# Interleaving the first convolution products with the input transposes, moving the token weights' low halves to VectorE, and splitting extra expert tiles two ahead

## The chip, the cores and the metric

The kernel runs on one core of one Trainium2 chip. A core has TensorE (PE: matmuls, and PEld: its weight loads), VectorE (DVE), ScalarE (ACT), GpSimd (POOL) and SyncE (SP, which here only issues DMAs). Each engine works through its own list of instructions in order; semaphores make one wait for another. The metric is the device time of one execution in microseconds (us); of several runs the median counts.

## What is computed

One step of a one-layer decoder over 1024 prompt tokens and 64 sample tokens, with 1024 channels. Cut to what the change touches:

```python
xn = rmsnorm(h, g_mix)
z = xn @ w_in                                  # columns: q, k, v, og, lr (tokens) and cv (convolution)
q, k, v, og, lr, cv = jnp.split(z, SPLITS, axis=-1)
...                                            # gated linear attention (GLA) from q, k, v, og, lr
a, gate = jnp.split(cv, 2, axis=-1)
u = a * jax.nn.sigmoid(gate)
c, buf_new = causal_depthwise_conv(u, buf0, w_conv, b_conv)     # 31 taps for each of 512 channels
c = jax.nn.silu(layernorm(c, g_conv_ln, b_conv_ln))
h = h + jnp.concatenate([o, c], axis=-1) @ w_out
xn = rmsnorm(h, g_ffn)
h = h + hier_moe(xn, ...)                      # 32 experts, two for each token
h = h + sigmoid(rmsnorm(h, g_ple) @ w_ple_gate) * (p_l @ w_ple_proj)
```

## The kernel before

The tokens are padded to 1152 and worked on in 9 tiles of 128. Products that need more accuracy than one 16-bit product are made of three: each operand is split into a high half (its value in 16 bits) and a low half (the rest), and the passes (high, high), (high, low), (low, high) are added up in PSUM. A split is thus two instructions: a copy (ACT) and a subtraction (DVE or POOL).

**Input stage.** For each tile SP loads 128 rows of x (`load_x`, two in flight), ACT squares and sums them, DVE normalises them (`norm_x`, L1244), PE turns them in eight transposes (`transpose_x`, L1718), ACT copies the high half out of PSUM (`evac_xT`, L892) and DVE subtracts for the low half (L1250). All of PE and DVE first wait for `g1_in`, which counts the load of the gains and of the whole table of constants (704.5 KB).

**Convolution products.** When all nine tiles are turned, PE multiplies four groups c of 128 channels (L1733): for each c two parts (gate and value), three blocks of 384 tokens, eight chunks of channels and three passes, 144 matmuls in all. The weights of a group (`w_cv`, 1 MB) come by DMA into one buffer; ACT makes the high half (L901) and POOL the low half (L713). ACT empties the six blocks of PSUM (L937: sigmoid of the gate, copy of the value) and POOL multiplies the two into `u` (L728, L729).

**Token weights.** The weights of q, k, v, og and lr come in eight chunks k of two halves (776 columns each) through two small buffers, `side`. For each half SP loads (L532), ACT makes the high part (L924), POOL the low part (L718), and only then may SP load the next chunk into that buffer (semaphore `wt_lo`). `w_pieces` puts chunks 0 to 2 into the list of group c=0, 3 to 5 into c=1, 6 and 7 into c=2, on SP, ACT and POOL alike; on ACT they stand ahead of the emptying of that group's PSUM.

**Depthwise taps.** DVE adds the 31 taps of each group to an accumulator, one instruction of 1024 columns each (`taps`: L1280 for the first, L1283 for the others), each waiting for the one before. Groups 0 and 1 get 22 taps ahead of the GLA loop; what is left (9 taps each, and all 31 of groups 2 and 3) is spread over eight GLA tiles, ten to a tile (`taps_beside`).

**GLA.** PE makes the token products of the next tile (`z`, L1741) between the small products of this one. The first tile's `cumulate` (L1773) waits for DVE's `log_gate` (L1304), which stands behind all taps of groups 0 and 1 in DVE's list.

**Experts.** 32 expert tiles and then up to 16 extra ones (five with these data) run through the same steps: gate and up products (`gate_up`, L1992), turning of the next rows, the down product of the tile before (L2010). In the regular tiles ACT and DVE split the weights of tile t+2 (`split_gu`, L1115 and L1576) during tile t. In an extra tile they split those of tile t+1.

## Time and profile before

| | us |
|---|---|
| median of 3 runs (1096.74 to 1102.41) | 1098.51 |
| the profiled execution | 1102.67 |
| its span, first to last instruction | 1100.8 |
| PE busy in it | 1005.0 (91%) |
| DVE busy | 711.0 (65%) |
| ACT busy | 475.6 (43%) |
| POOL busy | 367.9 (33%) |

Times inside the kernel are counted from the first instruction. Busy time of PE is drawn from matmuls that overlap, so that a row of a busy PE says little by itself; the rows that tell most are those with an idle time in front, and the distance from one start to the next. Lines (L1733) are those of the kernel before; in the changed kernel the same work stands some lines further on.

### The profile page before, as it was taken

The numbers are of one execution on the slowest core, as the hardware profiler recorded it, in microseconds if no ns is written. First come the engines' busy times: TensorE is split into PE (matmuls) and PEld (weight loads), VectorE is DVE, ScalarE is ACT, GpSimd is POOL, SyncE is SP. The second block draws the span as 40 slices with busy tenths as digits, with TensorE's granted clock in tenths as the row PEclk, the third lists the DMA queues.
The fourth block names the chain that finished last, engine by engine and source line by source line (L and its number), as shares of the span: only waits on it lengthen the run. The fifth ranks groups of instructions, "written<-read, shape, count | busy, mean of one in ns | idle before, by whom it ended". The sixth has DMA issues, their size and how long they took to land.

```text
span 1100.8 us, 14965 instructions
## 1 busy us (share of the span) xinstructions
PE 1005.0 (91%) x4992; PEld 544.9 (49%) x4992; DVE 711.0 (65%) x749; ACT 475.6 (43%) x656; POOL 367.9 (33%) x336
## 2 busy tenths in 40 slices
PE   4899979999999897999988999999999998748995
PEld 3555535555555564555534545555545543324442
DVE  6249865777776687444397877777777766437662
ACT  6333122322233533333254656555556645215664
POOL 0477233656631442111003433443433431101121
PEclk9999989999999899899999999999999999959998
DMA  7444040000000242222668999999999998252542
GB/s 259 120 128 142 1 21 1 1 1 0 0 0 1 78 139 77 85 86 84 218 278 314 408 415 382 354 363 360 393 371 367 371 370 296 99 212 77 181 163 76
DMA packets 54508, 200.59 MB, mean 182 GB/s; under 512 B 19567, under 2 KB 20864, under 8 KB 39490
## 3 DMA queue, kind: packets, MB, share of 16 engines
q1 hardware_dynamic: 42514, 177.47, 45.3%
q0 software_dynamic: 10656, 17.86, 4.3%
q10 hardware_dynamic: 1296, 4.72, 1.1%
q8 instruction: 24, 0.39, 0.1%
q14 instruction: 18, 0.15, 0.0%
HBM read 185.16 MB, written 35.81 MB: 201 GB/s over the span
## 4 chain that ended last, share of the span: by engine, by line
PE 68%; DVE 17%; DMA 5%; issue 4%; ACT 3%; POOL 1%; DVEq 1%; POOLq 0%; SPq 0%; ACTq 0%
PE psum L1992 18%; PE psum L1741 12%; PE psum L2010 10%; PE psum L1885 7%; DVE arena L1283 7%; PE psum L2060 4%; PE psum L1979 3%; DMA arena<-in_x 2%; DVE arena L1576 2%; PE psum L1868 2%; PE psum L1942 1%; DMA arena<-yrows 1%; PE psum L1808 1%; DMA arena<-in_w_cv 1%; PE psum L1807 1%
## 5 line engine op out<-in xcount | busy, mean ns | idle before, releaser
L1992 PE MATMUL psum<-arena 128*128 128x512 f16 x888 | 197.8, 379 | 11.2 <-DVE arena L1576 7.6
L1283 DVE SCALAR_TENSOR_TENSOR arena<-arena,wc x120 | 186.1, 1551 | 17.3 <-DVE arena L1283 17.0
L1576 DVE SCALAR_TENSOR_TENSOR arena<-arena 128x2048 f16<-128x2048 f32 x74 | 168.6, 2287 | 20.4 <-ACT arena L1115 20.3
L1741 PE MATMUL psum<-arena 128*128 128x512 f16 (+1 forms) x864 | 154.3, 333 | 0.6 <-ACT arena L937 0.6
L1992 PEld LDWEIGHTS psum<-arena 128*128 128x128 f16 x888 | 86.3, 98 | 109.8 <-DVE arena L1576 8.7
L1115 ACT ACTIVATE arena<-arena 128x2048 f16<-128x2048 f32 x74 | 140.0, 1902 | 1.1 <-ACT arena L1097 0.8
L835 POOL DMA_INDIRECT yrows<-tmp,idy x37 | 79.3, 2144 | 177.0 <-DVE tmp L1596 172.6
L2010 PE MATMUL psum<-arena 128*128 128x512 f32 x296 | 133.3, 593 | 1.3 <-DVE arena L1590 1.2
L1741 PEld LDWEIGHTS psum<-arena 128*128 (+1 forms) x864 | 68.5, 98 | 79.4 <-issue 10.7
L1733 PE MATMUL psum<-arena 128*128 128x384 f16 x576 | 96.5, 331 | 5.7 <-ACT arena L937 3.0
L1885 PE MATMUL psum<-arena 128*128 128x512 f16 x432 | 97.8, 384 | 0.8 <-DVE arena L1414 0.8
L2010 PEld LDWEIGHTS psum<-arena 128*128 128x128 f32 x296 | 53.4, 190 | 55.0 <-issue 54.8
L1733 PEld LDWEIGHTS psum<-arena 128*128 128x128 f16 x576 | 57.0, 99 | 45.3 <-issue 6.2
L1581 DVE TENSOR_TENSOR arena<-psum,arena 128x1024 f16<-128x1024 f32 x37 | 45.3, 1224 | 38.0 <-ACT arena L1120 38.0
L1979 PE MATMUL psum<-cst,arena 128*128 128x128 f32 x368 | 48.9, 277 | 20.5 <-DVE arena L1661 20.1
L1885 PEld LDWEIGHTS psum<-arena 128*128 128x128 f16 x432 | 42.7, 100 | 49.6 <-issue 2.4
L1126 ACT ACTIVATE arena<-psum 128x256 f32<-128x256 f32 x37 | 14.2, 384 | 118.8 <-PE psum L1992 118.8
L1979 PEld LDWEIGHTS psum<-cst,arena 128*128 128x128 f32 x368 | 43.3, 143 | 31.7 <-DVE arena L1661 20.9
L873 POOL TENSOR_TENSOR arena<-arena 128x1024 f32<-128x1024 f32 x9 | 21.1, 2342 | 109.3 <-DVE arena L1671 109.3
L2060 PE MATMUL psum<-tmp,arena 128*128 128x512 f16 x216 | 52.1, 393 | 2.5 <-DVE arena L1665 2.5
L824 POOL DMA_INDIRECT arena<-xn,idx x37 | 41.7, 1128 | 33.8 <-POOL idx L821 32.7
L742 POOL TENSOR_TENSOR tmp<-tmp,EL 64x512 f32<-64x512 f32 x8 | 17.5, 2187 | 96.7 <-DVE tmp L1331 59.1
(251 smaller groups left out, 1359.6 us busy)
## 6 DMA issues: line engine op xcount, KB each, us to landing
arena<-in_w_gu SPq DMA_DIRECT2D x74, 1024.0 KB, 9.5
arena<-in_w_dn SPq DMA_DIRECT2D x37, 1024.0 KB, 8.1
arena<-yrows SPq DMA_DIRECT2D x27, 512.0 KB, 5.4
side<-in_w_tok SPq DMA_DIRECT2D x16, 388.0 KB, 3.4
arena<-in_x SPq DMA_DIRECT2D x9, 512.0 KB, 4.7
side<-in_x SPq DMA_DIRECT2D x9, 512.0 KB, 4.0
xn<-arena SPq DMA_DIRECT2D x9, 512.0 KB, 2.9
out_y<-arena SPq DMA_DIRECT2D x9, 512.0 KB, 2.9
```

The costliest lines, as they stand in the source:

```text
L835: pl.indirect_dma_start(a["yrows"], bass.IndirectOffsetOnAxis(idy[sl][:], 0), yt[sl], None, bounds_check=2 * TOK, oob_is_err=False).then_i ...
L1115: act.activation(wgu[sl][0][:, 4 * u:4 * u + 4, :], raw[sl][:, 4 * u:4 * u + 4, :], ACT.Copy, scale=WS).then_inc(gu_hi, 1)
L1283: dve.scalar_tensor_tensor(acc, src, w[:, k:k + 1], acc, ALU.mult, ALU.add).then_inc(conv, 1)
L1576: dve.scalar_tensor_tensor(wgu[sl][1][:, 4 * u:4 * u + 4, :], raw[sl][:, 4 * u:4 * u + 4, :], WS, wgu[sl][0][:, 4 * u:4 * u + 4, :], ALU.m ...
L1581: dve.tensor_tensor(xgT[sl][1], psum[:, 0:2, :].rearrange("p a (b c) -> p (a b) c", c=P), xgT[sl][0], ALU.subtract).then_inc(xgT_v, 1)
L1733: x = pe.matmul(psum[:, 3 * part + b, 0:BLK], wcv[c % 2][w][:, k, col:col + P], xnT[m][:, k, b * BLK:(b + 1) * BLK], start=k + w + m == 0, ...
L1741: x = pe.matmul(out, xnT[w][:, k, bass.ds(n * P, P)], wtok[m][:, k, col:col + width], start=k + w + m == 0, stop=k == KC - 1 and w == 1)
L1885: x = pe.matmul(psum[:, 2 * j + half, :], catT[j][w][:, k, :], wout[m][:, k, half * 512:(half + 1) * 512], start=k + w + m == 0, stop=k == ...
L1979: x = pe.transpose(psum[:, k // 4, (k % 4) * P:(k % 4 + 1) * P], src[:, k * P:(k + 1) * P], ident)
L1992: x = pe.matmul(psum[:, 2 + sl, :], xgT[sl][w][:, k, :], wgu[sl][m][:, k, :], start=k + w + m == 0, stop=k == KC - 1 and w == 1)
L2010: x = pe.matmul(psum[:, 6 + half, :], hT[:, k, :], wdn[sl][:, k, half * 512:(half + 1) * 512], start=k == 0, stop=k == FC - 1)
L2060: x = pe.matmul(psum[:, 2 + 4 * j + half, :], x3T[j][w][:, k, :], wgate[k][m][:, 0, half * 512:(half + 1) * 512], start=k + w + m == 0, st ...
```

## The change

- SP loads the gains and only the identity (128 columns of the constants) ahead of the tiles, the weights of the first convolution group between tiles 2 and 3, and the rest of the constants behind the last tile. PE waits for the identity, DVE for the gains.
- POOL, not ACT, makes the high half of the first group's weights, as soon as they are there; the low half follows when all tiles are normalised.
- PE starts group 0 after the transposes of tile 4: its passes with the weights' high half are cut into 48 pieces of two matmuls; 5, 5, 6, 5 and 11 of them stand behind the transposes of tiles 4 to 8, 16 behind the last. The passes with the low half follow. The order of the other groups becomes blocks outside, parts inside, and the last block has 320 columns instead of 384 (`BW`: the padded tokens are left out).
- The low parts of the token weights move from POOL to DVE: chunks 0 to 2 ahead of the taps, 3 to 5 between the taps of group 0 (ahead of taps 4, 8, 12), 6 and 7 between those of group 1 (ahead of taps 4 and 8). On ACT the high parts are spread over the blocks: one chunk ahead of the emptying of each block.
- 18 taps of groups 0 and 1 (not 22) stand ahead of the GLA loop, eleven (not ten) beside each GLA tile; there the old group's and the new group's taps alternate, and an alternating tap waits for the tap before the last.
- ACT and DVE split the weights of the extra tiles two ahead, too. SP's list for the extra tiles is as before.
- Some semaphores are merged (`xn2_rdy`, `xn3_rdy` and others become later counts of `xs_rdy`, `xT_ps`, `xnT_a`, `xnT_v`); this moves nothing.

```diff
             load_x(0, 0)
             sp.dma_start(g1[:], a["g_mix"].to_broadcast([P, D])).then_inc(g1_in, 16)
-            sp.dma_start(cst[:], a["consts"]).then_inc(g1_in, 16)
+            sp.dma_start(cst[:, 0:P], a["consts"][:, 0:P]).then_inc(id_in, 16)
             load_x(1, 1)
-            with sp.Fori(1, (NT - 1) // 2) as i:
+            load_x(2, 0)
+            sp.dma_start(wcv_raw, a["w_cv"][0]).then_inc(wcv_in, 16)
+            load_x(3, 1)
+            with sp.Fori(2, (NT - 1) // 2) as i:
...
+            sp.dma_start(cst[:, P:CONST_W], a["consts"][:, P:CONST_W]).then_inc(c_in, 16)
...
+            sp.wait_ge(xs_rdy, NT - 1)
+            load_wt(0, 0)
+            load_wt(0, 1)
             for c in range(CC):
                 if c + 1 < CC:
                     sp.wait_ge(wcv_lo, c + 1)
                     sp.dma_start(wcv_raw, a["w_cv"][c + 1]).then_inc(wcv_in, 16)
-                w_pieces(sp, c, load_wt)
+                for k in range(3 * c + (c == 0), min(3 * c + 3, KC)):
+                    load_wt(k, 0)
+                    load_wt(k, 1)
...
-            split_cv(0)
+            pl.wait_ge(wcv_in, 16)
+            pl.tensor_copy(wcv[0][0], wcv_raw).then_inc(wcv_hi, 1)
+            pl.wait_ge(xs_rdy, NT)
+            split_cv(0)
             for c in range(CC):
                 if c + 1 < CC:
                     split_cv(c + 1)
-                w_pieces(pl, c, split_wt)
...
                 if c + 1 < CC:
                     split_cv(c + 1)
-                w_pieces(act, c, split_wt)
-                if c >= 1:
-                    act.wait_ge(u_rdy, 2 * c)
-                for part, (dst, fn) in enumerate([(sg_sb, ACT.Sigmoid), (a_sb, ACT.Copy)]):
-                    for b in range(NBLK):
-                        act.wait_ge(cv_ps, 6 * c + 3 * part + b + 1)
-                        act.activation(dst[:, b * BLK:(b + 1) * BLK], psum[:, 3 * part + b, 0:BLK], fn).then_inc(cv_sb, 1)
+                for b in range(NBLK):
+                    if 0 < 3 * c + b < KC:
+                        split_wt(3 * c + b, 0)
+                        split_wt(3 * c + b, 1)
+                    if c and not b:
+                        act.wait_ge(u_rdy, 2 * c)
+                    for part, (dst, fn) in enumerate([(sg_sb, ACT.Sigmoid), (a_sb, ACT.Copy)]):
+                        act.wait_ge(cv_ps, 6 * c + 2 * b + part + 1)
+                        act.activation(dst[:, b * BLK:b * BLK + BW[b]], psum[:, 2 * b + part, 0:BW[b]], fn).then_inc(cv_sb, 1)
...
+            REST = 13
+            PRE = K - REST
+            for k in range(3):
+                split_wt(k)
+            for c in range(2):
+                for k in range(PRE):
+                    if k in (4, 8, 12)[:3 - c]:
+                        split_wt(3 + 3 * c + k // 4 - 1)
+                    tap(c, k, PRE * c + k)
...
+            for n in range(4, NT):
+                transpose_x(n, n % 2)
+                if n == 4:
+                    pe.wait_ge(wcv_hi, 1)
+                conv_high((0, 5, 10, 16, 21)[n - 4], (5, 10, 16, 21, 32)[n - 4])
             pe.wait_ge(xnT_v, NT)
+            conv_high(32, 48)
             for c in range(CC):
                 pe.wait_ge(wcv_lo, c + 1)
-                for part, col in enumerate([P, 0]):
-                    for b in range(NBLK):
-                        if c >= 1:
-                            pe.wait_ge(cv_sb, 6 * (c - 1) + 3 * part + b + 1)
+                for b in range(NBLK):
+                    for part in range(2):
+                        if c == 0:
+                            conv_part(c, b, part, range(KC), PASSES[2:3])
+                        else:
+                            pe.wait_ge(cv_sb, 6 * (c - 1) + 2 * b + part + 1)
+                            conv_part(c, b, part, range(KC), PASSES)
...
                 silu(t + NE, sl)
                 with act.If(count > t + 1):
                     xgT_out(t + NE + 1, 1 - sl)
-                    split_gu(t + NE + 1, 1 - sl, 0)
-                    split_gu(t + NE + 1, 1 - sl, 1)
+                with act.If(count > t + 2):
+                    split_gu(t + NE + 2, sl, 0)
                 y_half(t + NE - 1, 1 - sl)
+                with act.If(count > t + 2):
+                    split_gu(t + NE + 2, sl, 1)
```

How the instructions stand is shown at three places. First TensorE in the input stage (L1718 before, L1738 now: transposes, eight to a tile; L1733 and L1744: convolution products). Before:

```order
L1718 MATMUL psum<-cst,arena 128x128 x16
L149 UNCONDITIONAL_BRANCH
...
L1718 MATMUL psum<-cst,arena 128x128 x8
L1714 REGISTER_ALU
L1718 MATMUL psum<-cst,arena 128x128 x8
L149 REGISTER_ALU
L149 COMPARE_AND_BRANCH
L1718 MATMUL psum<-cst,arena 128x128 x8
L1733 MATMUL psum<-arena 128x384 x576
```

And TensorE at the same place in the changed kernel, from the start to the first group's low passes:

```order
L1738 MATMUL psum<-cst,arena 128x128 x40
L1744 MATMUL psum<-arena 128x384 x10
L1738 MATMUL psum<-cst,arena 128x128 x8
L1744 MATMUL psum<-arena 128x384 x10
L1738 MATMUL psum<-cst,arena 128x128 x8
L1744 MATMUL psum<-arena 128x384 x12
...
L1738 MATMUL psum<-cst,arena 128x128 x8
L1744 MATMUL psum<-arena 128x384 x22
L1744 MATMUL psum<-arena 128x320 x32
L1744 MATMUL psum<-arena 128x384 x32
L1744 MATMUL psum<-arena 128x320 x16
```

Of the 576 products 64 now stand between the transposes of tiles 4 to 8 and 32 directly behind them, and a third of all is 320 columns wide.

Second, VectorE from the end of the input stage to the GLA loop, in the changed kernel (L1276: low parts of the token weights; L1287 and L1290: taps; L1319: `log_gate` of the first GLA tile). Before, no low part stood there, and 44 taps.

```order
L1276 TENSOR_TENSOR arena<-side,arena 128x776 [waits wt_hi] x6
L1287 TENSOR_SCALAR arena<-arena,wc,cvec 128x1024 [waits u_rdy]
L1290 SCALAR_TENSOR_TENSOR arena<-arena,wc 128x1024 [waits conv] x3
L1276 TENSOR_TENSOR arena<-side,arena 128x776 [waits wt_hi] x2
L1290 SCALAR_TENSOR_TENSOR arena<-arena,wc 128x1024 [waits conv] x4
...
L1287 TENSOR_SCALAR arena<-arena,wc,cvec 128x1024 [waits u_rdy]
L1290 SCALAR_TENSOR_TENSOR arena<-arena,wc 128x1024 [waits conv] x3
L1276 TENSOR_TENSOR arena<-side,arena 128x776 [waits wt_hi] x2
L1290 SCALAR_TENSOR_TENSOR arena<-arena,wc 128x1024 [waits conv] x4
L1276 TENSOR_TENSOR arena<-side,arena 128x776 [waits wt_hi] x2
L1290 SCALAR_TENSOR_TENSOR arena<-arena,wc 128x1024 [waits conv] x10
L1319 SCALAR_TENSOR_TENSOR tmp<-psum,tmp 128x256 [waits absx_rdy,y_zero]
```

The low part of chunk 6 (the first L1276 row behind the second L1287) now stands behind 22 taps, that of chunk 7 behind 26.

Third, ScalarE in the body of an extra expert tile (L1126 and L1123: silu; L1120 and L1117: the next rows; L1115 and L1112: high halves of expert weights; L1132 and L1129: half of the tile's result). Before:

```order
L1126 ACTIVATE arena<-psum 128x256 [waits gu_ps]
L1177 REGISTER_ALU
L1177 COMPARE_AND_BRANCH
L1119 REGISTER_ALU
L1120 ACTIVATE arena<-psum 128x1024 [waits xgT_ps]
L1112 ISA
L1114 REGISTER_ALU [waits gu_in00]
L1115 ACTIVATE arena<-arena 128x2048 [waits gu_ps]
L1115 ACTIVATE arena<-arena 128x2048 [waits gu_ps,gu_in01]
L1177 UNCONDITIONAL_BRANCH
L1129 REGISTER_ALU
L1131 ISA [waits y_ps]
```

ScalarE at the same place in the changed kernel:

```order
L1123 ACTIVATE arena<-psum 128x256 [waits gu_ps]
...
L1117 ACTIVATE arena<-psum 128x1024 [waits xgT_ps]
L1177 UNCONDITIONAL_BRANCH
...
L1112 ACTIVATE arena<-arena 128x2048 [waits gu_ps,gu_in10]
L1179 UNCONDITIONAL_BRANCH
...
L1129 ACTIVATE tmp<-psum 128x512 [waits y_out0]
...
L1112 ACTIVATE arena<-arena 128x2048 [waits gu_ps,gu_in11]
L1182 UNCONDITIONAL_BRANCH
```

The two high halves are now those of the tile after the next, and the tile's result stands between them.

## Rows read from the trace of the kernel before

**Rows 1.** The page: busy us of each engine (share of span), instructions.

```profile
PE 1005.0 (91%) x4992; PEld 544.9 (49%) x4992; DVE 711.0 (65%) x749; ACT 475.6 (43%) x656; POOL 367.9 (33%) x336
```

**Rows 2.** Stretches from:to; length, busy by engine (instructions), granted clock, DMA, GB/s.

```profile
170.00:371.00 201.00, 201.00 (x1160) 112.52 (x1158) 139.17 (x156) 56.47 (x109) 88.80 (x65) 0.97 0.00 0
...
590.00:889.00 299.00, 297.06 (x1291) 151.31 (x1290) 219.49 (x187) 174.73 (x157) 114.05 (x121) 1.00 0.97 376
```

**Rows 3.** Timeline, input stage: start, length, engine, instruction, [idle before, releaser].

```profile
8.24 0.16 DVE L1240 RECIPROCAL rst<-std 128x1 f32<-128x1 f32 x1 [8.24 <-DMA cst<-in_consts]
...
20.91 1.97 PE L1718 MATMUL psum<-cst,arena 128*128 128x128 f32 x8 [0.71 <-DVE arena L1250]
```

**Rows 4.** Timeline of PE, convolution products to first GLA tile.

```profile
36.23 25.94 PE L1733 MATMUL psum<-arena 128*128 128x384 f16 x144 [2.73 <-POOL arena L713]
63.74 23.56 PE L1733 MATMUL psum<-arena 128*128 128x384 f16 x144 [1.57 <-ACT arena L937]
88.75 46.96 PE L1733 MATMUL psum<-arena 128*128 128x384 f16 x288 [1.44 <-ACT arena L937]
136.29 5.96 PE L1741 MATMUL psum<-arena 128*128 128x16 f16 x48 [0.58 <-ACT arena L937]
...
143.34 5.35 PE L1741 MATMUL psum<-arena 128*128 128x512 f16 x24
156.44 1.22 PE L1773 MATMUL psum<-tmp,cst 128*128 128x256 f32 x2 [7.75 <-DVE tmp L1304]
...
158.54 8.03 PE L1741 MATMUL psum<-arena 128*128 128x512 f16 x24
```

**Rows 5.** Timeline of PEld, the first convolution products (one weight load for each).

```profile
40.67 0.15 PEld L1733 LDWEIGHTS psum<-arena 128*128 128x128 f16 x1 [0.17 <-issue]
40.99 19.01 PEld L1733 LDWEIGHTS psum<-arena 128*128 128x128 f16 x117 [0.17 <-issue]
```

**Rows 6.** Timeline of DVE, taps ahead of the GLA loop.

```profile
68.62 4.19 DVE L1280 TENSOR_SCALAR arena<-arena,wc,cvec  x1 [31.98 <-POOL arena L729]
...
91.51 3.12 DVE L1283 SCALAR_TENSOR_TENSOR arena<-arena,wc  x1 [0.18 <-DVE arena L1283]
94.81 5.11 DVE L1283 SCALAR_TENSOR_TENSOR arena<-arena,wc  x1 [0.18 <-DVE arena L1283]
...
126.23 1.29 DVE L1283 SCALAR_TENSOR_TENSOR arena<-arena,wc  x1 [0.18 <-DVE arena L1283]
```

**Rows 7.** Timeline of POOL, the operations beside those taps.

```profile
68.19 4.07 POOL L713 TENSOR_TENSOR arena<-arena 128x2048 f16<-128x2048 f32 x1
...
90.58 2.97 POOL L728 TENSOR_TENSOR arena<-arena 128x1024 f32<-128x1024 f32 x1 [0.33 <-ACT arena L937]
```

**Rows 8.** Groups by line and shape: busy us, mean ns | idle before.

```profile
L1361 DVE TENSOR_TENSOR arena<-arena 128x1024 f16<-128x1024 f32 x4 | 5.0, 1286 | 0.0
...
L797 POOL CAST arena<-arena 128x512 f16 x6 | 3.7, 610 | 66.1 <-PE psum L1885 66.1
```

**Rows 9.** ACT's timeline, and DMA issues: count, KB each, median us to landing.

```profile
104.88 0.85 ACT L924 ACTIVATE arena<-side 128x776 f32 x1 [9.70 <-DMA side<-in_w_tok]
...
side<-in_w_tok SPq DMA_DIRECT2D x16, 388.0 KB, 3.4
```

**Rows 10.** PE, end of GLA: an idle time (timeline), and the clock behind it (stretch).

```profile
423.12 2.16 PE L1911 MATMUL psum<-tmp,arena 128*64 128x128 f32 x10 [4.80 <-DVE arena L1414]
...
423.00:430.00 7.00, 6.25 (x40) 0.76 0.44 150
```

**Rows 11.** Waits of DVE in 170 to 371: us in total, times, longest.

```profile
DVE tmp L1331 <- PE psum L1811: 31.7, 8, 4.8
```

**Rows 12.** Chain of waits: starts of `gate_up` (start, length); the last is the fifth extra.

```profile
879.62 5.18 PE psum L1992 x24
...
889.33 5.18 PE psum L1992 x24
...
946.49 5.35 PE psum L1992 x24
```

More of the change, by code:

```diff
@@ L1139, in split_ple, with split_ahead @@
                 act.activation(wgate[k][0][:, 0, :], wple[k % 2], ACT.Copy).then_inc(wl_hi, 1)
+            def split_ahead(t, sl, u):
+                if isinstance(t, int) and t >= NE - 2:
+                    with act.If(count > t + 2 - NE):
+                        split_gu(t + 2, sl, u)
+                    hold(act, passed)
+                else:
+                    split_gu(t + 2, sl, u)
             def expert(t, sl):
@@ L1269, in _, with split_wt, tap @@
             dve.wait_ge(zero, 1)
[L1270 removed]
+            def split_wt(k):
+                for half in range(2):
+                    dve.wait_ge(wt_hi, 2 * k + half + 1)
+                    hi, lo = [w[:, k, half * TH:(half + 1) * TH] for w in wtok]
+                    dve.tensor_tensor(lo, wt_raw[half], hi, ALU.subtract).then_inc(wt_lo, 1)
+            def tap(c, k, done):
                 w = wc[:, bass.ds(c, 1), :].rearrange("p a k -> p (a k)")
                 acc = cT[:, bass.ds(c, 1), 0:SEQ].rearrange("p a t -> p (a t)")
[L1275 to L1283 removed]
@@ L1285, in _ @@
[L1285 to L1300 removed]
+                src = u[:, bass.ds(c, 1), k:k + SEQ].rearrange("p a t -> p (a t)")
@@ new lines, in _, with taps_beside @@
+            BESIDE = (K + REST) // 4
+            for k in range(3):
[5 more added lines that the diff above has]
+                    tap(c, k, PRE * c + k)
+            def taps_beside(i, first, count):
+                base = 2 * PRE + (K + REST) * i
+                for p in range(first, first + count):
+                    if p < 2 * REST and p % 2 == 0:
+                        tap(i, PRE + p // 2, base + p - 1 if p else PRE * i + PRE)
+                    elif p < 2 * REST:
+                        tap(i + CC // 2, p // 2, base + p - 1)
+                    else:
+                        tap(i + CC // 2, p - REST, base + p)
@@ L1600, in split_ple, with split_ahead @@
                 dve.tensor_tensor(wgate[k][1][:, 0, :], wple[k % 2], wgate[k][0][:, 0, :], ALU.subtract).then_inc(wl_lo, 1)
+            def split_ahead(t, sl, u):
+                if isinstance(t, int) and t >= NE - 2:
+                    with dve.If(count > t + 2 - NE):
+                        split_gu(t + 2, sl, u)
+                    hold(dve, passed)
+                else:
+                    split_gu(t + 2, sl, u)
             def expert(t, sl):
@@ new lines, in _, with conv_high @@
+            pieces = [(b, part, k) for b in range(NBLK) for part in range(2) for k in range(KC)]
+            def conv_high(first, last):
+                for b, part, k in pieces[first:last]:
+                    conv_part(0, b, part, [k], PASSES[0:2])
+            for n in range(4):
+                transpose_x(n, n % 2)
+            for n in range(4, NT):
+                transpose_x(n, n % 2)
+                if n == 4:
+                    pe.wait_ge(wcv_hi, 1)
+                conv_high((0, 5, 10, 16, 21)[n - 4], (5, 10, 16, 21, 32)[n - 4])
```

158 lines of the change are left out of this document (63 added, 95 removed).

## Prediction

> **What bounds the kernel now.** I read the page first: PE is busy for 91% of the span [rows 1], so a gain has to come from PE's own work, from its clock, or from the few places where it waits. The stretches say where these are not: in the GLA loop (170 to 371) PE is busy all the time and DVE for 69% of it, in the regular expert tiles PE is busy for 297 of 299 us [rows 2]. A faster DVE or ACT changes nothing there. The timelines show three places where PE is held up. In the input stage nothing starts before the constants have landed at 8.24, and PE only turns tiles: the reader is to see eight transposes in 1.97 us and the wait for DVE ahead of them [rows 3]. The convolution products begin at 36.23, last until 136.29 with short waits between the groups [rows 4], and their first 4.8 us run at half pace: a product of 384 columns each 0.32 us, then each 0.163 [rows 5] (columns per ns: the 1.2 GHz level, then the 2.4 GHz level). Then the first GLA tile: PE waits 7.75 us for DVE's `log_gate`, which stands behind 44 taps, and the gate product behind that wait takes 8.03 us where its like took 5.35 [rows 4]. Last, the extra expert tiles: starts are 9.71 us apart before them and (946.49 - 889.33) / 5 = 11.43 us in them [rows 12], since in an extra tile the splits of the next one's weights begin only after this one's products. All three are touched.
>
> **Sums go against the profiled execution** (1102.67 us, span 1100.8). It is 4.16 us over the median of the runs shown; I take the same gain off the median.
>
> **Start of the convolution.** The first tile no longer waits for the whole table of constants, but the 1 MB of weights now comes ahead of tile 3, and from there on tiles are paced as before. So the transposes of tile 4, at 20.91 before [rows 3], begin between 19 and 21; I take 20. From there PE has a stream without gaps. Two tiles of transposes at 1.97 make 3.9; 15 products at 0.32 make 4.8, as before the clock rose; 49 at 0.164 make 8.0. Three more tiles of transposes cost 5.9 at the pace of [rows 3], half of that if the risen clock halves them; I take 3.0, because products double their pace [rows 5]. The third block has 32 products of 320 columns, 0.164 x 320 / 384 = 0.136 each (an estimate by columns): 4.4. Sum 24.1: the high passes end at 44.1. The low passes, 32 x 0.164 + 16 x 0.136 = 7.4, end at 51.5. POOL's cast of the first weights costs, by 512 columns in 0.61 us [rows 8], some 2.4 us alone and up to twice that beside DVE; it is over before tile 4 is turned, so it costs PE nothing. DVE loses at most those microseconds, and PE, now behind its own stream, covers them.
>
> **Three groups more** are 96 x 0.164 + 48 x 0.136 = 22.3 us each, where 23.5 to 25.9 stood [rows 4], and follow without gaps, since a block's PSUM was emptied long before. That gives 51.5 + 66.8 = 118.3, and 0.6 for the last emptying: PE would begin the token products at 118.9 instead of 136.29.
>
> **The new wait.** But the loads of the token weights now form a ring: SP loads chunk k+1 only when DVE has made the low part of chunk k; that part stands among the taps; and on ACT the high part of chunk k+1 stands ahead of the emptying of a convolution block. Behind chunk 7 on ACT is the emptying of group 2, block 1, and PE needs that bank for group 3, block 1. I follow the ring.
> - Group 0: the low passes of block 0 end at 44.1 + 2.6 = 46.7, emptied at 47.2; chunk 1 on ACT 1.7 (two of 0.85 [rows 9]); low part 1.0; load of chunk 2 3.4 [rows 9]; chunk 2 on ACT 1.7; two emptyings 1.0: 56.0. The gating product on POOL, 2.97 [rows 7], gives `u` at 59.0 (68.62 before [rows 6]).
> - DVE then does 22 taps at 1.29 + 0.18 [rows 6]: 32.3. Seven low halves of 776 columns, by 1286 ns for 1024 [rows 8], are 0.97 each: 6.8. Beside them lie the same POOL operations as before, which made single taps 4.19, 3.12 and 5.11 long [rows 6, 7]: 2.9 + 1.8 + 3.8 = 8.5 more. POOL's fourteen low parts between them are gone. So the low half of chunk 6 is done at 59.0 + 47.6 = 106.6.
> - Chunk 7 lands at 110.0; ACT 1.7 and the emptying 0.5: 112.2. PE arrives at 51.5 + 44.6 + 48 x 0.164 = 104.0 and waits 8.2 us.
>
> After an idle time like that the clock is lower for a while: behind 4.80 us of idle the granted clock was 0.76 for 7 us, which is 3.4 us at half pace and costs 1.7 [rows 10]; behind 7.75 us one product group cost 8.03 - 5.35 = 2.7 [rows 4]. I take 2.5. The wait costs 10.7 in all, and PE begins at 129.6: 6.7 earlier than before. From below this can be 0 (rival A), from above see the last rival.
>
> **First GLA tile.** Ahead of it DVE has 36 taps (52.9), ten low halves (9.7) and the POOL operations (8.5, and 1.8 for each of two more): done at 59.0 + 74.7 = 133.7. PE wants `log_gate` 143.34 + 5.35 - 136.29 = 12.4 us after its start [rows 4], at 142.0. The 7.75 us go, and with them the slow product: 7.75 + 2.7 = 10.4. What is late next is PE itself.
>
> **GLA loop.** An eleventh tap adds 1.47 us to each tile, alternating takes 0.18 off some. It stands ahead of the state update, where DVE waited 31.7 us in eight tiles, 4.0 each [rows 11]; so it costs nothing. With that cover gone it would be up to 8 x 1.47 = 12.
>
> **Extra tiles.** ACT and DVE do in an extra tile what they do in a regular one, and PE's order is the same; so the period becomes 9.71: 5 x 1.72 = 8.6. The cover is in the weights' loads, whose issue stays where it was, behind the down product, a little later than in regular tiles. If they land late, the gain shrinks towards 0. Branches cost ACT and DVE something; both have 2 to 4 us to spare in 9.71 [rows 2]. Merged semaphores and the late constants cost nothing: they land while PE is still in group 0.
>
> **Sum:** 6.7 + 10.4 + 8.6 = 25.7. 1102.67 - 25.7 = 1077.0 for the profiled execution, 1098.51 - 25.7 = 1072.8 for the median: 1073.
>
> **Rivals.**
> - A, the ring is quick enough and PE doesn't wait in group 3. For it: most taps ahead of the loop will meet no POOL operation; 8 us less in a ring of 47.6 are enough. Against: three of them will, and nothing else in the ring is optional. Then PE starts at 118.9, 10.7 more gain, 1062. Chance 0.24.
> - B, the clock stays at its lower level until the last transposes. For it: nine tiles of transposes, 9 x 1.97 = 18 us of PE work, stood ahead of 36.23 and the products still began at 0.32 [rows 3, 5]; now less than two thirds of the stream between tiles 4 and 8 are products. Of the 42 products there 27 cost 0.156 more (4.2), three tiles of transposes 2.9, and 15 products behind them 2.3: 9.4, 1082. Chance 0.13. The Trainium skill, TensorE: Matmul & The Clock Gate, Part 4: PE-mode transpose, states that the full clock doesn't engage for transposes, as they do not count as busy in the same way; by that rule this rival is the case, and the trace agrees as far as pure transposes go.
> - C, the extra tiles keep their period, since ACT waits for the weights' loads: 25.7 - 8.6 = 17.1 gain, 1081. Against: the loads have one tile's time to land. That the splits don't come two ahead at all would look the same. Chance 0.10.
> - D, slower: the ring is far longer, as every tap ahead of chunk 6 meets POOL or is held up otherwise. Each us on a tap is 22 us on the wait. The gain is used up at (47.6 + 25.7 - 6.8) / 22 = 3.0 us for a tap; at 3.5 the time is 1072.8 + 22 x 3.5 + 6.8 - 47.6 = 1109. For it: single taps of 3.12 and 5.11 [rows 6]. Against: these lay beside POOL operations of 3 to 4 us, and few are left. Chance 0.03 for slower, 0.03 for a gain that is nearly gone.
>
> **How the numbers follow.** The forecast keeps 0.47; its own range is 1066 to 1080 (start of the stream +-1, wait 4 to 12, its clock cost 1.7 to 3.8, extras 6 to 8.6). To hold 8 in 10 the range takes in A with 2 us below it and B and C at its upper end: 1060 to 1083. A measurement of this kernel can tell about 0.5%, 5.5 us, from no change. Faster by more than that are the forecast, A, B, C and small mishaps: 0.94. Within 0.5%: D at 2.8 to 3.3 us for a tap, 0.03. Slower: 0.03.
>
> **What would show it.** Right: products of 384 columns between transposes from about 22; `u` of group 0 at 55 to 60; one wait of PE for ACT of 5 to 10 us in the middle of group 3, with a lower granted clock behind it; token products at 126 to 132; no wait ahead of `cumulate`; starts of extra tiles 9.7 apart. Wrong: no wait in group 3 (A); 0.32 us products up to tile 8 (B); extra tiles over 11 us apart, with ACT waiting for DMA (C); a state update that PE waits for in the GLA loop (the cover of the eleventh tap is gone); taps of over 3 us in series (D).

## The result

The changed kernel takes 1069.57 us (median, 1066.38 to 1070.0); the kernel before, run on the same chip, takes 1097.93 us. The ratio is 0.9732, 95% interval 0.9709 to 0.9755: 28.4 us less. The forecast was 1073 in a range of 1060 to 1083, faster. Its direction and size hold. By the profiles, the terms up to the first GLA tile gave more than forecast and the extra tiles less; that the median came so near is in part luck, as the section on the prediction shows.

### The profile page after: what moved, and what is told of

Read it like the earlier page. It is cut to its first block, busy times and chain, and to the rows that moved or that the text cites. A ratio compares the mean times of both kernels' runs of the same rounds, so it can differ in the third digit from the quotient of the medians.

```text
span 1068.2 us, 14779 instructions
## 1 busy us (share of the span) xinstructions
PE 989.3 (93%) x4992; PEld 541.2 (51%) x4992; DVE 707.4 (66%) x765; ACT 473.8 (44%) x655; POOL 364.7 (34%) x321
## 4 chain that ended last, share of the span: by engine, by line
PE 74%; DVE 14%; DMA 5%; issue 3%; ACT 2%; SPq 1%; POOL 0%; POOLq 0%; DVEq 0%; ACTq 0%
PE psum L2030 17%; PE psum L1779 13%; PE psum L2048 11%; PE psum L1923 8%; PE psum L2098 5%; DVE arena L1290 4%; PE psum L2017 3%; PE psum L1744 3%; DMA arena<-yrows 2%; PE psum L1906 2%; PE psum L1980 1%; PE psum L1846 1%; PE psum L1845 1%; DMA arena<-in_w_gu 1%; PE psum L1849 1%
## 5 line engine op out<-in xcount | busy, mean ns | idle before, releaser
L1290 DVE SCALAR_TENSOR_TENSOR arena<-arena,wc (+1 forms) x120 | 169.5, 1432 | 6.1 <-DVE arena L1290 5.1
L1112 ACT ACTIVATE arena<-arena 128x2048 f16<-128x2048 f32 x74 | 140.6, 1903 | 15.6 <-DMA arena<-in_w_gu 14.7
L829 POOL DMA_INDIRECT yrows<-tmp,idy x37 | 85.3, 2305 | 169.8 <-DVE tmp L1611 159.2
L1744 PE MATMUL psum<-arena 128*128 128x384 f16 (+1 forms) x576 | 91.9, 322 | 5.3 <-ACT arena L934 5.3
L1744 PEld LDWEIGHTS psum<-arena 128*128 128x128 f16 x576 | 57.1, 99 | 38.8 <-ACT arena L934 5.7
L1123 ACT ACTIVATE arena<-psum 128x256 f32<-128x256 f32 x37 | 14.2, 384 | 96.8 <-PE psum L2030 96.8
L735 POOL TENSOR_TENSOR tmp<-tmp,EL 64x512 f32<-64x512 f32 x8 | 33.3, 4166 | 63.1 <-DVE tmp L1346 38.2
L818 POOL DMA_INDIRECT arena<-xn,idx x37 | 41.7, 1128 | 33.7 <-POOL idx L815 32.6
```

Of the source, the lines that this page charges most:

```text
L829: pl.indirect_dma_start(a["yrows"], bass.IndirectOffsetOnAxis(idy[sl][:], 0), yt[sl], None, bounds_check=2 * TOK, oob_is_err=False).then_i ...
L1112: act.activation(wgu[sl][0][:, 4 * u:4 * u + 4, :], raw[sl][:, 4 * u:4 * u + 4, :], ACT.Copy, scale=WS).then_inc(gu_hi, 1)
L1290: dve.scalar_tensor_tensor(acc, src, w[:, k:k + 1], acc, ALU.mult, ALU.add).then_inc(conv, 1)
L1744: x = pe.matmul(psum[:, 2 * b + part, 0:BW[b]], wcv[c % 2][w][:, k, P * (1 - part):P * (2 - part)], xnT[m][:, k, b * BLK:b * BLK + BW[b]], ...
```

## The profile after

The profiled execution took 1070.0 us (span 1068.2). That of the kernel before was 4.7 us over the median of its runs here, so the two profiles differ by 32.6 us where the medians differ by 28.4. PE is busy for 989.3 us of it (93%), against 1005.0 us (91%) in [rows 1].

**Input stage** (timeline of PE: start, length, instruction, [idle before, releaser]; then one stretch, with the granted clock as third number from the end), against [rows 3, 5]:

```profile
20.16 1.94 PE L1738 MATMUL psum<-cst,arena 128*128 128x128 f32 x8 [0.79 <-DVE arena L1253]
21.90 2.69 PE L1744 MATMUL psum<-arena 128*128 128x384 f16 x10
24.42 1.04 PE L1738 MATMUL psum<-cst,arena 128*128 128x128 f32 x8
25.29 1.79 PE L1744 MATMUL psum<-arena 128*128 128x384 f16 x10
...
33.11 67.50 PE L1744 MATMUL psum<-arena 128*128 128x384 f16 x438
```

```profile
22.00:24.00 2.00, 2.00 (x9) 0.97 (x8) 1.75 (x3) 1.76 (x2) 0.00 (x0) 1.00 0.92 246
```

The first ten products take 2.69 us, the next ten 1.79: the pace doubles within the first ten (0.32 to 0.163 us each, the 1.2 and the 2.4 GHz level), and the transposes double with them, 1.94 to 1.04. The granted clock reads 1.00 here although the products still take 0.32 us, so that in this stretch the level is read from the pace, not from that column. From 20.16 to 100.61 PE has no gap.

**Convolution to the first GLA tile** (timeline of PE), against [rows 4]:

```profile
105.93 16.01 PE L1744 MATMUL psum<-arena 128*128 128x384 f16 x96 [5.32 <-ACT arena L934]
122.47 5.96 PE L1779 MATMUL psum<-arena 128*128 128x16 f16 x48 [0.53 <-ACT arena L934]
...
134.71 0.60 PE L1811 MATMUL psum<-tmp,cst 128*128 128x256 f32 x2
...
135.79 5.35 PE L1779 MATMUL psum<-arena 128*128 128x512 f16 x24
141.07 0.43 PE L1823 MATMUL psum<-cst,tmp 128*64 128x128 f32 x2
```

One wait is left, of 5.32 us for ACT, in the middle of group 3. The token products start at 122.47 (136.29 before). `cumulate` (L1811) waits for nobody, and the gate product behind it takes 5.35 us where 8.03 stood. The first turn of q and k (L1823) comes at 141.07, where 166.50 stood in the trace of before: 25.4 us. ACT's timeline and the granted clock of two stretches show where the 5.32 us come from and what follows them:

```profile
102.76 0.85 ACT L916 ACTIVATE arena<-side 128x776 f16<-128x776 f32 x1 [15.63 <-DMA side<-in_w_tok]
104.64 0.85 ACT L916 ACTIVATE arena<-side 128x776 f16<-128x776 f32 x1 [1.03 <-DMA side<-in_w_tok]
105.40 1.50 ACT L934 ACTIVATE arena<-psum 128x384 f32<-128x384 f32 x4
```

```profile
105.90:108.00 2.10, 2.07 (x7) 1.04 (x8) 2.10 (x3) 1.00 (x3) 1.02 (x1) 0.50 0.00 0
108.00:110.00 2.00, 2.00 (x11) 1.04 (x9) 2.00 (x1) 0.00 (x0) 2.00 (x2) 0.74 0.00 0
```

ACT waited 15.63 us for the first half of chunk 7, and behind chunk 7 stands the emptying (L934) of the bank that PE wants. After the wait some nine products ran at 0.32 us: 9 x 0.156 = 1.4 us.

**DVE's taps** (timeline), against [rows 6]:

```profile
55.98 0.81 DVE L1287 TENSOR_SCALAR arena<-arena,wc,cvec 128x1024 f32<-128x1024 f32 x1 [2.52 <-POOL arena L722]
...
66.28 5.24 DVE L1290 SCALAR_TENSOR_TENSOR arena<-arena,wc 128x1024 f32<-128x1024 f32 x4
...
98.50 1.84 DVE L1276 TENSOR_TENSOR arena<-side,arena 128x776 f16<-128x776 f32 x2
...
133.57 0.42 DVE L1319 SCALAR_TENSOR_TENSOR tmp<-psum,tmp 128x256 f32<-128x256 f32 x1 [11.15 <-ACT tmp L951]
```

Four taps take 5.24 us, 1.31 each, not 1.29 + 0.18. The low halves of chunk 6 start at 98.50. The 36 taps end at 133.57 - 11.15 = 122.4, long before `log_gate` (L1319) has its operand.

**GLA loop and regular experts.** From the first to the last turn of q and k it is 204.6 us in both traces, with one tap more in each tile; from the first to the last regular expert start it is 299.8 us in both. DVE still waits 19.4 us for PE ahead of the state update in eight tiles, where [rows 11] had 31.7: the cover of the eleventh tap has shrunk, not gone.

**Extra tiles** (timelines of PE, SP's queue and ACT), against [rows 12]:

```profile
862.85 5.34 PE L2030 MATMUL psum<-arena 128*128 128x512 f16 x24
...
882.26 5.34 PE L2030 MATMUL psum<-arena 128*128 128x512 f16 x24
...
894.09 5.35 PE L2030 MATMUL psum<-arena 128*128 128x512 f16 x24 [0.19 <-DVE arena L1596]
...
913.51 5.34 PE L2030 MATMUL psum<-arena 128*128 128x512 f16 x24
```

```profile
872.69 0.34 SPq L652 DMA_DIRECT2D arena<-in_w_dn  x1
874.46 1.14 SPq L646 DMA_DIRECT2D arena<-in_w_gu  x2
```

```profile
884.59 1.91 ACT L1112 ACTIVATE arena<-arena 128x2048 f16<-128x2048 f32 x1 [4.76 <-DMA arena<-in_w_gu]
```

Four of five periods are 9.7 us, one is 11.83. In that one ACT waited 4.76 us for weights that SP had issued at 874.46, behind a down load that waits for an earlier down product. From the last regular start (862.85) to the last extra one (913.51) it is 50.66 us. In [rows 12] it was 57.16, but the chain of waits puts the start of the last regular tile later than the timeline does, which reads for the kernel before:

```profile
889.17 5.34 PE L1992 MATMUL psum<-arena 128*128 128x512 f16 x24
```

Timeline against timeline it was 946.49 - 889.17 = 57.32 us, so the change is worth 6.7 us here.

## The experiments

The theory after these rows: (a) a denser start of the convolution, (b) no late `log_gate` and no slow products behind it, (c) shorter extra tiles; and two remains, the wait of 5.3 + 1.4 us in group 3 and the late load in the extra tiles, 2.1 us. All kernels below are edits of the changed one (1069.57, ratio 0.9732, token products at 122.47). The ratio is to the kernel before in the same comparison; its interval is 2 to 4.5 us to either side.

| kernel | median us | ratio, 95% interval | token products from |
|---|---|---|---|
| e_ring | 1063.47 | 0.9693, 0.9670 to 0.9716 | 115.71 |
| e_ring_rest9 | 1071.25 | 0.9770, 0.9732 to 0.9807 | 116.61 |
| e_rest9 | 1070.62 | 0.9770, 0.9730 to 0.9811 | 123.48 |
| e_pool_low | 1076.64 | 0.9810, 0.9788 to 0.9831 | 120.22 |
| e_extras_old | 1074.26 | 0.9773, 0.9749 to 0.9797 | 123.87 |
| e_both | 1062.86 | 0.9673, 0.9654 to 0.9693 | 116.42 |
| e_no_interleave | 1075.78 | 0.9799, 0.9774 to 0.9824 | 129.67 |
| e_ring_no_int | 1070.48 | 0.9748, 0.9720 to 0.9776 | 122.69 |
| e_rolled | 1073.92 | 0.9782, 0.9755 to 0.9809 | 127.05 |
| e_ring_wide | 1068.12 | 0.9717, 0.9691 to 0.9743 | 121.65 |
| e_best | 1060.34 | 0.9655, 0.9630 to 0.9679 | 115.58 |

### The wait in group 3: e_ring

```diff
-                    if k in (4, 8, 12)[:3 - c]:
-                        split_wt(3 + 3 * c + k // 4 - 1)
+                    at = ((4, 8, 12, 16), (2,))[c]
+                    if k in at:
+                        split_wt(3 + 4 * c + at.index(k))
```

> Edit: DVE makes the low parts of token-weight chunks 6 and 7 earlier, behind taps 16 and 20 of its first 36 instead of 22 and 26; the number of operations is the same. Theory (PE's wait of 5.32 us in the middle of group 3 of the convolution comes from the ring load, ACT's high half, DVE's low half, and its length is set by how many taps stand ahead of the low half of chunk 6): the low half of chunk 6 comes 6 x 1.31 = 7.9 us earlier, so chunk 7 passes ACT at 97.5 instead of 105.4, ahead of PE's arrival at 100.6. The wait goes (5.3) and with it the slow products behind it (1.4): 6.7 us less than the changed kernel, 1063, token products from 115.8. log_gate brings no new wait, since DVE's taps end at 122.4 and ACT is done at 126.9. Rival 1 (the ring is set by the loads or by ACT): the wait stays at 4 to 5 us, 1069. Rival 2 (DVE only shifts its work, and log_gate becomes late): the wait goes in group 3 and comes back ahead of cumulate, 1068 to 1070.

Timelines of PE and ACT in e_ring:

```profile
94.69 20.50 PE L1745 MATMUL psum<-arena 128*128 128x384 f16 x133
115.71 5.96 PE L1780 MATMUL psum<-arena 128*128 128x16 f16 x48 [0.53 <-ACT arena L934]
```

```profile
95.45 1.80 ACT L916 ACTIVATE arena<-side 128x776 f16<-128x776 f32 x2 [9.81 <-DMA side<-in_w_tok]
97.16 1.51 ACT L934 ACTIVATE arena<-psum 128x384 f32<-128x384 f32 x4
```

The wait is gone, chunk 7 leaves ACT at 97.2 (97.5 was worked out), the token products start at 115.71 against 115.8 forecast, and the first turn of q and k moves from 141.07 to 134.32. The time is 1063.47. Same work in another place: the wait came from where the low halves stood among the taps, and nothing swallowed the gain.

### How many taps ahead: e_ring_rest9 and e_rest9

```diff
-            REST = 13
+            REST = 9
```

e_ring_rest9 has the placing of e_ring besides; in e_rest9 the low parts of chunks 6 and 7 stay behind 22 and 26 taps.

> Edit: as e_ring, and 44 taps ahead of the GLA loop with 10 in each of its tiles, as in the kernel before, instead of 36 and 11. Theory (once the wait in group 3 is gone, PE reaches log_gate of the first tile so early that the number of taps ahead decides): DVE ends 8 x 1.31 = 10.5 us later, at 132.9, against 126.9 for ACT, so PE waits 6.0 us ahead of cumulate, and the products behind it are slow for some 2 us more: 8 us above e_ring, 1071. Rival (the taps were not the cause of the wait of 7.75 us in the kernel before, POOL's contention was): no difference from e_ring, 1063.

> Edit: 44 taps ahead of the GLA loop and 10 in each of its tiles, as before the change, instead of 36 and 11; the low parts stand behind as many taps as in the changed kernel, so the ring is the same. Theory: the wait in group 3 holds PE up as long as before, DVE ends its taps at 122.4 + 8 x 1.31 = 132.9, and ACT brings its part for log_gate only at 133.57: no difference, 1069.5 (0 to 1 us more). That would mean that the move of eight taps into the loop brings nothing in this kernel as it stands. Rival, the step of the prediction that gave 10.4 us to the shorter row of taps: a wait of 7.75 us and 2.7 us of slow products come back, 1080.

e_rest9: 1070.62, no difference that can be told; its `cumulate` has no wait in front, though only just: `log_gate` follows the last tap at once. e_ring_rest9: 1071.25, 7.8 us above e_ring. PE's timeline there shows the old picture of [rows 4] again:

```profile
136.36 1.22 PE L1812 MATMUL psum<-tmp,cst 128*128 128x256 f32 x2 [7.35 <-DVE tmp L1320]
...
138.47 6.96 PE L1780 MATMUL psum<-arena 128*128 128x512 f16 x24
```

So eight taps more in the loop bring nothing in the changed kernel, where the wait in group 3 makes PE as late as the longer row of taps would. They bring 8 us as soon as that wait is gone. In the changed kernel, taking taps out was not what removed the late `log_gate`.

### Where the low halves are made: e_pool_low

```diff
+                for k in range(3 * c, min(3 * c + 3, KC)):
+                    for half in range(2):
+                        pl.wait_ge(wt_hi, 2 * k + half + 1)
+                        ...
+                        pl.tensor_tensor(lo, wt_raw[half], hi, ALU.subtract).then_inc(wt_lo, 1)
                 pl.wait_ge(cv_sb, 6 * (c + 1))
```

with `split_wt` taken out of DVE's list.

> Edit: the low parts of the token weights are made on POOL again, behind the low part of the next convolution weights, and no longer among DVE's taps. Theory (DVE's low parts close the ring behind a row of taps; on POOL they close it at once): a chunk takes load 3.4, ACT 1.7 and POOL 3.3 us, 8.4 or less as its halves overlap, near a block's 7.4 us, so the wait in group 3 goes nearly. DVE loses 10 low parts of 0.97 among the taps and pays 10 x 1.65 us of POOL time beside which a tap takes 2.42 instead of 1.31, 7.6 us: its taps end about where they did. Sum 0 to 7 us less than the changed kernel, 1063 to 1070. Rival (the low parts were the reason that taps took 2.42 us, and u is late behind them): u of the groups comes 3 to 6 us later, PE waits between groups as in the kernel before (1.5 us each) and at log_gate: 1073 to 1080.

1076.64: the rival holds in the main. Timelines of POOL, ACT, DVE and PE:

```profile
45.21 3.27 POOL L724 TENSOR_TENSOR arena<-side,arena 128x776 f16<-128x776 f32 x2
...
61.15 2.36 POOL L726 TENSOR_TENSOR arena<-arena 128x1024 f32<-128x1024 f32 x1
63.47 0.32 POOL L727 TENSOR_TENSOR arena<-arena 128x64 f32<-128x64 f32 x1
```

```profile
59.36 0.75 ACT L939 ACTIVATE arena<-psum 128x320 f32<-128x320 f32 x2
```

```profile
68.41 42.82 DVE L1295 SCALAR_TENSOR_TENSOR arena<-arena,wc 128x1024 f32<-128x1024 f32 x17
```

```profile
95.20 9.65 PE L1745 MATMUL psum<-arena 128*128 128x384 f16 x48 [2.00 <-POOL arena L710]
105.20 14.49 PE L1745 MATMUL psum<-arena 128*128 128x384 f16 x96 [0.34 <-ACT arena L939]
...
137.23 1.22 PE L1812 MATMUL psum<-tmp,cst 128*128 128x256 f32 x2 [4.61 <-DVE tmp L1320]
...
139.33 7.22 PE L1780 MATMUL psum<-arena 128*128 128x512 f16 x24
```

The wait for ACT in group 3 shrank to 0.34 us, as the theory had it (another of 2.00 us, for POOL's low half of that group's weights, stands one block earlier). But `u` (L726, L727) is ready at 63.8 instead of 55.9, and 17 taps beside POOL's operations take 42.82 us, 2.52 each. `log_gate` is late again. Most of the delay of `u` comes through the ring: on POOL the low halves of chunk 0 stand behind the low half of the next convolution weights and start at 45.21 (36.12 on DVE in the changed kernel), so chunk 2 is late, and the emptying behind it on ACT ends at 60.1 instead of 53.1. Only 1.0 us is POOL's own low half right in front of `u`. The theory had left out what stands ahead of the low halves in POOL's list. Against this order on POOL, which is that of the kernel before, the move to DVE is worth 7 us, by shorter taps and an earlier `u`, although it costs DVE ten low parts among the taps. Low halves on POOL ahead of the convolution weights were not run.

### The head start: e_no_interleave and e_ring_no_int

```diff
-                if n == 4:
-                    pe.wait_ge(wcv_hi, 1)
-                conv_high((0, 5, 10, 16, 21)[n - 4], (5, 10, 16, 21, 32)[n - 4])
+            pe.wait_ge(wcv_hi, 1)
+            conv_high(0, 32)
```

> Edit: the changed kernel with all convolution products behind the last transpose. Theory (part of the head start is swallowed by the ring of the token weights): the high passes end 10 us later (42 products of 0.164 no longer lie between the transposes, and 15 products take 0.32 again), at 51.7; the first group's u comes at 62.4 instead of 55.9, since it had been held by the chunks of the token weights anyway; chunk 7 passes ACT at 105.4 + 6.5 = 111.9, PE arrives at 111.1. The wait of 5.3 and its slow products 1.4 go nearly, so the token products begin 4 to 5 us later only: 1074. Rival (the interleaving brings its whole head start): 10.5 us more, 1080.

> Edit: e_ring with all convolution products behind the last transpose. Theory: with the ring's wait gone nothing swallows the head start any more, so PE's token products begin the whole 10 us later than in e_ring, at 126: 1073.5, about as late as without interleaving in the changed kernel. Rival (the interleaving is worth the same with and without the ring's wait): 4 to 5 us more than e_ring, 1068, or 10 in both.

1075.78 and 1070.48: 6.2 and 7.0 us above the changed kernel and e_ring, 7.2 and 7.0 in the start of the token products. PE in e_no_interleave, from the last eight transposes on:

```profile
30.66 1.83 PE L1738 MATMUL psum<-cst,arena 128*128 128x128 f32 x8 [0.58 <-DVE arena L1253]
32.33 74.32 PE L1744 MATMUL psum<-arena 128*128 128x384 f16 x480
111.84 17.30 PE L1744 MATMUL psum<-arena 128*128 128x384 f16 x96 [5.19 <-ACT arena L934]
```

My idea that the ring swallows part of the head start falls: without interleaving PE arrives at group 3, block 1, at 106.65, 6.0 us later, and `u` of the first group at 61.97, also 6.0 later, so the wait keeps its length (5.19). The other 1.2 us of the 7.2 lie behind the wait, where 96 products take 17.30 us instead of 16.01. The expected delay of 10 us was too long: products began at 32.33 with none at 0.32, and 64 x 0.164 + 32 x 0.136 = 14.9 us of high passes end at 47.2, not at 51.7. The interleaving is worth 6 to 7 us, ring or no ring. PEld in e_no_interleave, and then in e_ring_no_int, at the first products:

```profile
32.18 17.75 PEld L1744 LDWEIGHTS psum<-arena 128*128 128x128 f16 x115
```

```profile
34.33 0.15 PEld L1745 LDWEIGHTS psum<-arena 128*128 128x128 f16 x1 [0.17 <-issue]
34.65 15.34 PEld L1745 LDWEIGHTS psum<-arena 128*128 128x128 f16 x100 [0.17 <-issue]
```

Up to there PE did the same in both, transposes alone. In the one the products run at full pace at once, and the last eight transposes ahead of them already took 1.83 us instead of 1.94; in the other the products take 0.32 us until 34.65.

### The pace of the taps: e_rolled

```diff
-            for k in range(3):
+            for k in range(2):
                 split_wt(k)
-            for c in range(2):
+            with dve.Fori(0, 2) as c:
                 for k in range(PRE):
-                    if k in (4, 8, 12)[:3 - c]:
-                        split_wt(3 + 3 * c + k // 4 - 1)
+                    if k in (0, 4, 8):
+                        split_wt(2 + 3 * c + k // 4)
```

> Edit: the changed kernel with DVE's first 36 taps written as a hardware loop of two rounds, as the taps ahead of the GLA loop were before the change; the low parts of chunks 6 and 7 stand behind the same number of taps, that of chunk 5 behind 18 instead of 12. Theory (the prediction's tap of 1.29 + 0.18 us was that of a hardware loop; written out, as the change has them, taps follow each other at 1.31): the 22 taps ahead of the low half of chunk 6 take 22 x 0.16 = 3.5 us more, PE's wait in group 3 is 8.8 instead of 5.3, near the 8.2 of the prediction, and the token products begin at 126: 1073. Rival 1 (the gap has another cause, what POOL does at the time): taps at 1.31, wait 5.3, 1069.6. Rival 2 (chunk 5, six taps later, takes the ring over): wait over 10 us, 1076.

1073.92. Timelines of DVE and PE:

```profile
70.20 1.29 DVE L1290 SCALAR_TENSOR_TENSOR arena<-arena,wc  x1 [0.18 <-DVE arena L1290]
...
101.52 1.83 DVE L1276 TENSOR_TENSOR arena<-side,arena 128x776 f32 x2
```

```profile
101.69 24.83 PE L1744 MATMUL psum<-arena 128*128 128x384 f16 x144 [7.89 <-ACT arena L934]
127.05 5.96 PE L1779 MATMUL psum<-arena 128*128 128x16 f16 x48 [0.53 <-ACT arena L934]
```

The gap of 0.18 us is back, taps come 1.47 apart, and PE's wait grows to 7.89 us. The gap comes with the loop form; whether the loop itself makes it, or the addresses and counts that are then held in registers, isn't told apart. In the ring it is worth less than the theory's 3.5 us: from `u` (56.66) to the end of chunk 6's first low half (102.4, half of the row at 101.52) it takes 45.8 us, 2.3 more than in the changed kernel (43.5). The gap isn't the only cause of the longer wait either: 144 products lie behind the wait, not 96, so PE waited one block earlier, for the emptying that stands behind chunk 6, which the later low part of chunk 5 held up. The size agrees with the theory partly by this second effect; the two aren't told apart.

### The narrower block: e_ring_wide

```diff
-        BW = [BLK] * (NBLK - 1) + [SEQ + NS - (NBLK - 1) * BLK]
+        BW = [BLK] * NBLK
```

> Edit: e_ring with the last block of the convolution 384 columns wide instead of 320, as before the change. Theory (products go by columns: 0.164 at 384, 0.136 at 320): 48 products in each of four groups, 4 x 48 x 0.027 = 5.2 us more, and nothing hides it, since PE is the bound once the ring's wait is gone: token products at 120.9, 1068.7. Rival 1 (the block's end is set by the emptying or by POOL, not by the columns): 0 to 2 us, 1064. Rival 2 (the later products let the ring or the taps matter again): over 7 us, 1071.

1068.12; the token products start at 121.65, 5.9 us later than in e_ring (5.2 forecast). Of these, 0.8 us lie ahead of the stream of products; the stream itself takes 86.94 us instead of 81.82. The narrower block is worth its columns.

### The extra tiles: e_extras_old, e_both, e_best

e_extras_old splits the weights of the extra tiles one tile ahead on ACT and DVE, as before. e_both is e_ring with

```diff
+                with sp.If(count > t + 2):
+                    extra_gu(t + 2, sl)
                 e = sp.value_load(plan[0:1, bass.ds(t, 1)], min_val=0, max_val=NE - 1)
                 sp.wait_ge(y_ps, t + NE - 1)
                 sp.dma_start(wdn[sl], ...)
-                with sp.If(count > t + 2):
-                    extra_gu(t + 2, sl)
```

and e_best has the line with `value_load` ahead of both.

> Edit: the changed kernel with the extra tiles' weights split one tile ahead, behind this tile's products, as before the change. Theory: the starts of the extra tiles are again (946.49 - 889.33) / 5 = 11.43 us apart instead of 10.13, 6.6 us more in five periods: 1076. Rival (part of the gain comes from the tail behind the last tile, where work was moved out): over 8 us more, 1078 and above; or the extras gained less and the start more: under 5 us, 1074.

> Edit: e_ring, and in an extra tile SP issues the gate and up weights of the tile two ahead before the down weights of this one, as it does in regular tiles. Theory (the period of 11.83 us among the extra tiles comes from the weights of extra tile 2, whose load was issued at 874.46 behind a down load that waits for an earlier down product, some 10 us too late, so that ACT waited 4.76 us for it): the load is issued a tile earlier, all five periods are 9.7 us, 2.1 us less than e_ring: 1061.4, and 8.8 us less than the changed kernel. Rival (the loads of an extra tile are late whatever their place, or the branches cost it): one or more periods stay above 11, no difference from e_ring, 1063.5.

> Edit: e_both with the number of this extra tile's expert read ahead of the gate and up loads, so that it no longer lies between them and the down load. Theory (in e_both the down weights of the first extra tile came 0.42 us too late, behind two reads of about 1.4 us): five periods of 9.71, 0.7 us less than e_both, 1062 within its noise; the row of the wait for the down weights is gone. Rival: the wait stays, as the issue waits for the gate and up weights' buffer, no difference.

PE in e_extras_old and in e_both, each from the last regular to the last extra start:

```profile
864.79 5.34 PE L2022 MATMUL psum<-arena 128*128 128x512 f16 x24
...
922.12 5.35 PE L2022 MATMUL psum<-arena 128*128 128x512 f16 x24 [1.58 <-DVE arena L1587]
```

```profile
857.31 5.34 PE L2031 MATMUL psum<-arena 128*128 128x512 f16 x24
...
873.65 3.67 PE L2049 MATMUL psum<-arena 128*128 128x512 f32 x8 [0.42 <-DMA arena<-in_w_dn]
...
906.50 5.34 PE L2031 MATMUL psum<-arena 128*128 128x512 f16 x24
```

e_extras_old: 57.33 us in five periods, as before the change (57.32) and 6.67 more than the changed kernel; the medians differ by 4.7, within what they can tell. e_both: 49.19 us, 1.5 less than e_ring's 50.73 (852.86 to 903.59); ACT's late load is gone, and a smaller one appears, 0.42 us for the down weights. e_best keeps it (0.40), so the read of the expert's number wasn't its cause; SP's queue shows the down load of e_both issued at 867.13, with the start of its tile, as in the changed kernel. That it is late because it now comes behind the gate and up weights in the queue is likely, but no run shows it. Medians: e_both 1062.86, e_best 1060.34, e_ring 1063.47; they don't tell these three apart. The rows show 1.5 us between e_ring and e_both and nothing between e_both and e_best (49.17). Both beat the changed kernel by 7 to 9 us.

No run takes out the new order of blocks and parts, or the early start of group 0's weights, by itself. The short waits between the groups [rows 4] are gone in the changed kernel; which of the edits removed them isn't shown.

## Why the prediction was right, and where it was off

- **Start.** Tile 4 at 20.16 (forecast 20). PE reached the middle of group 3 at 100.6 instead of 104.0: the pace doubled within the first ten products, not after 15, and four tiles of transposes took 1.04, not only three at about half. Rival B is out. The Trainium skill, TensorE: Matmul & The Clock Gate, Part 4: PE-mode transpose, says that the full clock does not engage for transposes; here transposes between products run at 1.04 instead of 1.94 us, and in e_no_interleave the first product behind transposes alone is at full pace, as the last transposes begin to be (1.83). The trace decides against the rule as stated.
- **The wait in group 3** was found where it was put, by the ring that was followed, and e_ring shows that ring to be its cause. Its size was 5.32 + 1.4 against 8.2 + 2.5: the tap of 1.29 + 0.18 came from rows of a hardware loop [rows 6], and the change writes taps out (1.31; e_rolled gives the 0.18 back). The ring was 4.1 us shorter than summed up (43.5 from `u` to the end of chunk 6's first low half, not 47.6); by e_rolled 2.3 of them are the gap, and the first tap of a group, 0.81 long instead of 1.29, and low halves of 0.92 instead of 0.97 make part of the rest.
- **First GLA tile.** Forecast 10.4, measured 11.6 (from the start of the token products to the first turn 30.2 before, 18.6 after). Of the 1.2 more, 1.0 are the small products behind `cumulate`, which were slow before (from its start to the gate product 2.10, then 1.08). The amount was right, and it would be so whatever brings `log_gate` ahead of PE; of the reason I gave only a part holds: I counted on 36 taps instead of 44, and e_rest9 has 44 without a wait. With the low parts on POOL even 36 taps end too late (e_pool_low); with them on DVE, and the taps written out, 44 are in time as long as the wait in group 3 is there.
- Both together: 25.4 us at the first turn of q and k, where the sum had 17.1.
- **GLA loop**, at nothing: right, 204.6 us before and after.
- **Extra tiles.** Forecast 8.6 with a lower bound of 6, measured 6.7. The stated risk, the issue of the loads "a little later than in regular tiles", cost 2.1 us in one tile; it was named, priced at nothing in the sum and covered only by the lower bound.
- **The sum** was 25.7. The terms up to the first GLA tile gave 8.3 more, the extras 1.9 less; 0.9 came from between GLA and experts, where the statistics products of the layer norm ran slower in the profile of before, and the tail behind the experts lost 0.4: 32.6, the difference of the profiles. The medians differ by 28.4. So the sum, which goes against the profile, was 6.9 too small, and the median came within 3.4 of the forecast because the profiled execution of the kernel before was also 4.7 over its median, a part that the median doesn't gain. That is luck. Where these 4.7 us lie stays open, since no other execution of the kernel before has a trace.
- Rivals A, C and D: PE did wait, the extra tiles got shorter, the 22 taps of the ring didn't come near 3 us each. A's condition (a ring some 8 us shorter) is what e_ring brings about by hand; A gave 1062, e_ring took 1063.5.

## What to carry to other kernels

When a small buffer goes round between a DMA queue and several engines, follow one turn of it through each engine's list and look for what stands behind it there; moving four subtractions ahead by six taps each was worth about as much (6 us) as any part of this change that was taken out by itself. Count an instruction's pitch from rows of the same form of code: a tap in a hardware loop and one written out differed by 0.16 us, and 22 taps lay on the path (2.3 us in e_rolled). And a gain upstream (fewer taps ahead, e_rest9) shows nothing until the wait behind it is taken away (e_ring_rest9); so try such edits in pairs.

## What the runs showed of the hardware that was not expected

- Products behind the same stretch of transposes started at 0.32 us in e_ring_no_int, until 34.65, and at full pace at once in e_no_interleave. Before the change, behind an idle time of 2.73 us, it took until 40.99 [rows 4, 5]. Among the kernels that interleave, the pace doubled between 1.2 us (e_pool_low) and 3.1 us (e_ring_rest9) behind the first product. The start of a stream can differ by over 2 us between executions with nothing changed ahead of it.
- Taps on DVE, each waiting for the one before, stand 0.18 us apart in a hardware loop and about 0.02 written out (taps of 1.28 to 1.29 us, 1.47 and 1.31 apart; e_rolled and the changed kernel).
- Beside POOL's operations in e_pool_low, 17 taps took 2.52 us each instead of 1.31. In the kernel before, the tap of 5.11 us [rows 6] starts at 94.81, 0.03 us behind the start of an operation of POOL:

```profile
94.78 4.07 POOL L713 TENSOR_TENSOR arena<-arena 128x2048 f16<-128x2048 f32 x1
```

The Trainium skill, SBUF — State Buffer, Summary: rules for kernel authors, says that a VectorE instruction with two inputs in SBUF and a GpSimd instruction that reads SBUF exclude each other, and that the later one waits for the whole of the other. The trace agrees: waiting for the rest of POOL's operation and then running alone makes 4.04 + 1.28 = 5.32 us (an estimate), 0.2 more than the 5.11 measured.
